# A planned order set to measured durations of products, and the decay matrices moved from VectorE to GpSimd and ScalarE

## The reference

```python
# first block
h = rms_norm(x); (aq,ak,av,az,dq,dk,dv,db,da,dz,gate_att,gate_dn) = split_cols(h @ w_in)
y_att = (gqa_attention(rope(norm(aq)), rope(norm(ak)), av) * silu(az)) @ w_br_att     # 8 heads, 2 kv heads
qkv = silu(short_conv([dq,dk,dv]))                                                      # 5 taps
g = -exp(a_log) * softplus(da + dt_bias); beta = sigmoid(db)                            # 2 directions, 8 heads
o_dn = gated_delta(q,k,v,g[0],beta[0]) + flip(gated_delta(flip q,k,v,g[1],beta[1]))     # chunks
  # in it: g = cumsum(g) per chunk
  #        decay = exp(where(tril, g[:, None] - g[None, :], -inf))
  #        L = tril((k_beta @ k.T) * decay, -1); T = (I + L)^-1; u, w, a_intra = (q @ k.T) * decay; scan over chunks
y_dn = (rms_norm(o_dn) * silu(dz)) @ w_br_dn
x = x + rms_norm((sigmoid(gate_att)*y_att + sigmoid(gate_dn)*y_dn) @ w_out)
x = x + rms_norm(sigmoid(x @ w_ple_gate) * (p @ w_ple_proj))
# second and third block
x = x + stick_breaking_attention(...)@w_out;  x = x + swiglu_ffn(rms_norm(x))           # 16 heads
x = x + (rms_norm(a1@v - lam*a2@v) per head)@w_out;  x = x + swiglu_ffn(rms_norm(x))    # differential attention, 8 heads
```

## Time and profile before

| | value |
|---|---|
| median of 3 runs (range) | 2147.75 us (2145.37 to 2148.02) |
| the profiled execution's own time | 2149.83 us |
| its span | 2148.0 us |
| granted clock of TensorE, mean | 0.997 |
| PE busy | 2104.3 us, 98% |
| DVE busy | 1275.4 us, 59% |
| ACT busy | 1054.6 us, 49% |
| POOL busy | 235.0 us, 11% |
| share of the ending chain: PE, DVE, ACT, issue | 89%, 6%, 3%, 1% |

### The profile page before, as it was taken

The page is one execution under the profiler, slowest core; times in us unless marked ns, Lnnn a source line. Parts: engine busy times, 40 slices in busy tenths (PEclk is TensorE's granted clock), DMA queues, the critical chain, the costliest instruction groups (busy, mean ns, idle before and its releaser), DMA issues.

```text
span 2148.0 us, 36022 instructions
## 1 busy us (share of the span) xinstructions
PE 2104.3 (98%) x15046; PEld 1680.9 (78%) x15046; DVE 1275.4 (59%) x2281; ACT 1054.6 (49%) x2046; POOL 235.0 (11%) x240
## 2 busy tenths in 40 slices
PE   7999999999999999999999999999999999999999
PEld 6777777787778887877777888888777777888887
DVE  6777677776755455655567443444577775443442
ACT  6656766676655236656665332323455554222331
POOL 1013222231210011100001000000100101000000
PEclk9999999999999999999999999999999999999999
DMA  4321212222224332111111332222221212232222
GB/s 179 108 75 62 77 68 85 68 77 65 71 80 147 127 137 95 60 59 59 59 59 64 101 114 81 98 98 98 84 64 64 64 59 99 98 103 94 98 100 77
DMA packets 36227, 186.76 MB, mean 87 GB/s; under 512 B 4560, under 2 KB 4944, under 8 KB 16992
## 3 DMA queue, kind: packets, MB, share of 16 engines
q1 hardware_dynamic: 36064, 184.45, 25.1%
HBM read 172.86 MB, written 7.90 MB: 84 GB/s over the span
## 4 chain that ended last, share of the span: by engine, by line
PE 89%; DVE 6%; ACT 3%; issue 1%; DMA 0%; SPq 0%; POOL 0%; DVEq 0%; ACTq 0%
PE ps L1879 87%; ACT arena L2841 1%; PE ps L1882 1%; DVE spl L2337 1%; ACT spl L2844 1%; ACT hh L2841 0%; DVE x L2706 0%; DMA raw<-wstream 0%; DVE x L2464 0%; DVE arena L2356 0%; DVE arena L2649 0%; DVE x L2635 0%; DVE arena L2631 0%; DVE hl L2657 0%; DVE hl L2639 0%
## 5 line engine op out<-in xcount | busy, mean ns | idle before, releaser
L1879 PE MATMUL ps<-hh,spl 128*128 128x512 f32 (+1 forms) x3152 | 1018.2, 396 | 10.9 <-ACT x L2844 2.1
L1879 PEld LDWEIGHTS ps<-hh,spl 128*128 128x128 f32 x3152 | 584.7, 189 | 144.7 <-issue 19.1
L1879 PE MATMUL ps<-hl,spl 128*128 128x512 f32 (+1 forms) x1568 | 616.0, 393 | 0.0
L2337 DVE TENSOR_TENSOR spl<-raw,spl 128x512 fp32r<-128x512 f32 x596 | 427.2, 740 | 159.1 <-ACT spl L2844 158.0
L1879 PE MATMUL ps<-arena_r,spl 128*128 128x512 f32 x1968 | 468.7, 393 | 10.4 <-DVE arena_r L2349 8.5
L1879 PEld LDWEIGHTS ps<-arena_r,spl 128*128 128x128 f32 x1968 | 371.9, 189 | 90.1 <-issue 10.9
L2844 ACT ACTIVATE spl<-raw 128x512 fp32r<-128x512 f32 x596 | 345.1, 619 | 144.4 <-PE ps L1879 138.2
L1879 PEld LDWEIGHTS ps<-hl,spl 128*128 128x128 f32 x1568 | 295.5, 188 | 60.6 <-issue 4.8
L2841 ACT ACTIVATE arena<-arena 128x512 f32<-128x512 f32 (+3 forms) x220 | 142.2, 648 | 187.3 <-DVE arena L2711 141.1
L1879 PE MATMUL ps<-arena 32*32 32x32 f32 (+5 forms) x5664 | 216.9, 224 | 7.5 <-issue 6.1
L1879 PEld LDWEIGHTS ps<-arena 32*32 32x32 f32 (+4 forms) x5664 | 126.1, 115 | 82.3 <-issue 70.6
(11 more groups left out here) (271 smaller groups left out, 2143.1 us busy)
## 6 DMA issues: line engine op xcount, KB each, us to landing
raw<-wstream SPq DMA_DIRECT2D x148, 1024.0 KB, 4.9
arena<-spill SPq DMA_DIRECT2D x17, 256.0 KB, 4.5
GS<-g_rows SPq DMA_DIRECT2D x16, 256.0 KB, 3.3
spill<-x SPq DMA_DIRECT2D x14, 256.0 KB, 2.6
arena<-arena SPq DMA_DIRECT2D x18, 128.0 KB, 2.0
x<-xT SPq DMA_DIRECT2D x4, 512.0 KB, 6.2
spill<-arena SPq DMA_DIRECT2D x8, 256.0 KB, 2.1
x<-xT SPq DMA_DIRECT2D x1, 2048.0 KB, 8.3
```

Source lines behind the costliest of these rows:

```text
L1879: return pe.matmul(out, lhsT, rhs, start=start, stop=stop, skip_group_check=True)
L2337: tt(spl[:, p % 2, 1, c], raw[:, p % 2, c], spl[:, p % 2, 0, c].bitcast(F32), ALU.subtract) \
```

## The change

Two parts. **First**, constants of the planner's clock. `CHANGE` was one number between "one pass" products and others; it becomes a table over three forms of product, WIDE (512 columns on the whole array), NARROW (128 columns) and TILED (parts of the array). The costs of about fifteen steps are set to other values, and three base values. **Second**, the decay matrices. Before, VectorE computed min(g_j - g_i, 0) with four TENSOR_SCALARs for each head and direction, ScalarE one exp over 128x512, and GpSimd multiplied by a triangular mask (L3278). After, GpSimd adds a mask of 0 and -1e30 to g_j (one instruction), and ScalarE computes exp(x - g_i) in four ACTIVATEs of 128x128 that take -g_i as bias; the gate column is negated once. The small copy `eglast` moves on GpSimd from `pr_e` to `pr_q`, and the scan's state update waits for `pr_q` in place of `pr_e`. The GpSimd step gets two new waits, since it now writes the buffers: for `pr_b` of the head before, and for the drained bank of `lv_q2` two heads back.

```diff
-PE_B, DV_B, AC_B, PO_B = 0.86, 0.69, 0.62, 1.25
-PE_S2 = 0.46
+PE_B, DV_B, AC_B, PO_B = 0.866, 0.69, 0.62, 1.25
+PE_S2 = 0.47
-PE_H, DV_H, AC_H = 0.44, 0.41, 0.37
+PE_H, DV_H, AC_H = 0.35, 0.41, 0.37
-CHANGE = 0.088
-ONE_PASS = ("mul", "tok", "ar_ss", "cv_r", "on_b", "st_w", "st_t")
+CHANGE = {(WIDE, TILED): 0.1, (NARROW, TILED): 0.1, (TILED, WIDE): 0.1, (TILED, NARROW): 0.05, (NARROW, WIDE): 0.06}
...
-            st = banked("df_s", m, qb, cost=[("PE", 0.15 + 0.86 * f), ("DV", 0.15 + 1.08 * f), ("AC", 0.25 + 0.42 * f),
+            st = banked("df_s", m, qb, cost=[("PE", 0.25 + 0.85 * f), ("DV", 0.15 + 1.08 * f), ("AC", 0.25 + 0.42 * f),
...
@@ rows_lane
-            yield "DV"
+            yield "AC"
             o.add("pr_a", hd, d, cost=[("AC", AC_B)])
-            yield "DV"
-            o.add("pr_g", hd, d, cost=[("DV", 4 * DV_S)]).ib = decays[hd]
+            yield
+            o.add("pr_g", hd, d, cost=[("PO", 1.4)]).ib = decays[hd]
...
-            yield
-            o.add("pr_e", hd, d, cost=[("AC", AC_B), ("PO", PO_B)]).ib = decays[hd]
+            yield "AC"
+            o.add("pr_e", hd, d, cost=[("AC", 4 * 0.36)]).ib = decays[hd]
@@ vector
-                elif kind == "pr_g":
-                    hd, d = q.key
-                    col = d * 8 + hd
-                    w.wait_ge(sem(f"g_ld{d}"), 16 * (hd + 1))
...
-                    for c in range(4):
-                        i = ts(g4(B_of[q.ib][d])[:, c, :], g4(GS[:, d, :])[:, c, :], g3(gcol)[:, c, col:col + 1], 0.0,
-                               ALU.subtract, ALU.min)
-                    i.then_inc(sem("pr_d"), 1)
...
-                        w.wait_ge(sem("pr_ld"), at["pr_e", hd, 1].n)
+                        w.wait_ge(sem("pr_qe"), at["pr_q", hd, 1].n)
@@ scalar, pr_e
-                    f(B_of[q.ib][d], B_of[q.ib][d], ACT.Exp).then_inc(sem("pr_ed"), 1)
...
+                    for c in range(4):
+                        b_, col = g4(B_of[q.ib][d])[:, c, :], d * 8 + hd
+                        i = f(b_, b_, ACT.Exp, bias=g3(gcol)[:, c, col:col + 1])
+                    i.then_inc(sem("pr_ld"), 1)
@@ gpsimd
-                elif kind == "pr_e":
+                elif kind == "pr_g":
                     hd, d = q.key
-                    e0, D = (d * 8 + hd) * 4, B_of[q.ib][d]
-                    w.wait_ge(sem("pr_eg"), at["pr_a", hd, d].n)
-                    po.tensor_copy(eglast[:, e0:e0 + 4], g4(G_of[d])[:, :, 127 if d == 0 else 0])
-                    w.wait_ge(sem("pr_ed"), q.n)
-                    tt(g4(D), g4(D), bc4(C["tri_u" if d == 0 else "tri_l"]), ALU.mult).then_inc(sem("pr_ld"), 1)
+                    w.wait_ge(sem(f"g_ld{d}"), 16 * (hd + 1))
+                    if hd > 1:
+                        w.wait_ge(sem("pr_b"), hd - 1)
+                        t = at["lv_q2", hd - 2].u
+                        w.wait_ge(drained[t.b], t.n)
+                    tt(g4(B_of[q.ib][d]), g4(GS[:, d, :]), bc4(C["off_u" if d == 0 else "off_l"]), ALU.add) \
+                        .then_inc(sem("pr_d"), 1)
```

More of the change, by code:

```diff
@@ L44 @@
 NVEC = _at
-PE_B, DV_B, AC_B, PO_B = 0.86, 0.69, 0.62, 1.25
-PE_S2 = 0.46
+PE_B, DV_B, AC_B, PO_B = 0.866, 0.69, 0.62, 1.25
+PE_S2 = 0.47
 PE_S, DV_S, AC_S, PO_S = 0.21, 0.34, 0.3, 0.6
 MUL, MUL_H = 0.228, 0.117
-PE_H, DV_H, AC_H = 0.44, 0.41, 0.37
+PE_H, DV_H, AC_H = 0.35, 0.41, 0.37
 HOP = 0.08
-CHANGE = 0.088
-ONE_PASS = ("mul", "tok", "ar_ss", "cv_r", "on_b", "st_w", "st_t")
+WIDE, NARROW, TILED = 0, 1, 2
+CHANGE = {(WIDE, TILED): 0.1, (NARROW, TILED): 0.1, (TILED, WIDE): 0.1, (TILED, NARROW): 0.05, (NARROW, WIDE): 0.06}
+FORM = {**dict.fromkeys(("at_o", "at_t", "sc_r", "sc_v", "sc_oq", "sc_s", "sc_o", "tr_k", "tr_v", "pr_kk", "df_t", "df_o"),
+                        NARROW),
+        **dict.fromkeys(("lv_m", "lv_x", "lv_p1", "lv_p2", "lv_q1", "lv_q2", "st_z", "st_o", "df_s"), TILED)}
 TAIL_32 = 0.4
@@ L141, in __init__ @@
         self.uses, self.fills, self.bank_free = [0] * 8, [0] * 8, [0.0] * 8
-        self.forced, self.aside = False, False
+        self.forced, self.form = False, WIDE
         self.lanes, self.later = {}, []
@@ L161, in add @@
             st.u, t = u, max(t, u.t)
-        if cost and cost[0][0] == "PE" and self.aside != (kind not in ONE_PASS):
-            self.aside = not self.aside
-            self.clock["PE"] += CHANGE
+        if cost and cost[0][0] == "PE":
+            form = FORM.get(kind, WIDE)
+            self.clock["PE"] += CHANGE.get((self.form, form), 0.0)
+            self.form = form
         for q, c in cost:
@@ L573, in att_lane @@
             if qb:
-                banked("at_t", hd, qb - 1, cost=[("PE", 0.45), ("AC", AC_B)])
+                banked("at_t", hd, qb - 1, cost=[("PE", 0.43), ("AC", AC_B)])
                 o.now = t
@@ L690, in conv_lane @@
                 yield "PE"
-            st = banked("tr_k", hd, cost=[("PE", 0.45), ("AC", AC_B)])
+            st = banked("tr_k", hd, cost=[("PE", 0.44), ("AC", AC_B)])
             st.keep = kept[hd]
@@ L742, in prep_lane @@
             yield "PE"
-        st = add("pr_kk", hd, cost=[("PE", 1.7), ("DV", 2 * DV_B), ("DV", 8 * DV_S)], hold=True)
+        st = add("pr_kk", hd, cost=[("PE", 1.82), ("DV", 2 * DV_B), ("DV", 8 * DV_S)], hold=True)
         st.u2 = ring.take()
@@ L801, in scan_lane @@
             if s > 0:
-                add("sc_r", s, [("PE", 0.43), ("DV", 2 * DV_S)])
+                add("sc_r", s, [("PE", 0.44), ("DV", 2 * DV_S)])
                 yield "PE"
             t = o.now
-            add("sc_v", s, [("PE", 0.43), ("AC", 0.72)])
+            add("sc_v", s, [("PE", 0.44), ("AC", 0.72)])
             if s > 0:
                 t, o.now = o.now, t
-                st = add("sc_oq", s, [("PE", 0.43)], False)
+                st = add("sc_oq", s, [("PE", 0.55)], False)
                 st.first, first, o.now = first, False, max(t, o.now)
@@ L812, in scan_lane @@
             if s < 3:
-                add("sc_s", s, [("PE", 0.43), ("DV", 2 * DV_S)])
+                add("sc_s", s, [("PE", 0.44), ("DV", 2 * DV_S)])
             t, o.now = o.now, t
-            st = add("sc_o", s, [("PE", 0.43)], False)
+            st = add("sc_o", s, [("PE", 0.46)], False)
             st.first, first, o.now = first, False, max(t, o.now)
@@ L1328, in stick_back @@
             z = o.at["st_z", m, kb]
-            st = last = o.add("st_w", m, kb, cost=[("PE", 0.1 + 0.92 * f)])
+            st = last = o.add("st_w", m, kb, cost=[("PE", max(0.45, 0.93 * f))])
             st.ih = o.at["st_h", m, kb].ih
@@ L1334, in stick_back @@
                 ut = obs.take()
-                last = o.add("st_t", m, kb, cost=[("PE", 0.1 + 0.92 * f)], u=ut)
+                last = o.add("st_t", m, kb, cost=[("PE", max(0.45, 0.93 * f))], u=ut)
                 last.u, last.isp, last.ih = ut, z.isp, st.ih
@@ L1509, in mix_lane @@
         yield "AC PE"
-        st = banked("df_o", m, cost=[("PE", 2.2), ("AC", AC_B), ("AC", AC_B)], bank=obk)
+        st = banked("df_o", m, cost=[("PE", 2.12), ("AC", AC_B), ("AC", AC_B)], bank=obk)
         st.iat, st.old = iat, on_old
@@ L3284, in gpsimd @@
                     w.wait_ge(sem("cv_n"), at["cv_n", hd].n)
-                    tt(keep_of[q.keep][f"qe{d}"], q_tile[hd % 2], G_of[d], ALU.mult).then_inc(sem("pr_qe"), 1)
+                    po.tensor_copy(eglast[:, e0:e0 + 4], g4(LG)[:, :, 127 if d == 0 else 0])
+                    tt(keep_of[q.keep][f"qe{d}"], q_tile[hd % 2], LG, ALU.mult).then_inc(sem("pr_qe"), 1)
                 elif kind == "lv_0":
@@ L3349, in shape_constants @@
          "neg_ones": -np.ones((128, 128), np.float32), "strict_u": one(r < c), "neg_lo": -1e30 * one(c >= r % 64),
-         "neg_hi": -1e30 * one(c >= 64 + r % 64), "rep64": one(c == r % 64)}
+         "neg_hi": -1e30 * one(c >= 64 + r % 64), "rep64": one(c == r % 64),
+         "off_u": -1e30 * one(r > c), "off_l": -1e30 * one(r < c)}
     lev = []
```

14 lines of the change are left out of this document (8 added, 6 removed).

## The result

The changed kernel takes 2170.73 us (median of 5 runs, 2167.0 to 2176.54) against 2148.02; the ratio is 1.0106, 95% interval 1.0093 to 1.0118. It is 22.7 us slower. 2155 was forecast and 2167 was the upper end: the direction was right, the size a third of what came. The profiled execution of the changed kernel took 2176.54 (span 2174.8), the slowest of the five, so a comparison of the two traces has 26.7 us to explain.

A forecast was written before the change was run, and what follows sets the result against it. TensorE, busy for 2104.3 of 2148.0 us, was taken as the bound, so only its gaps counted. The terms summed to +7.6: 2157.4 for the profiled execution, 2155 us against the medians, range 2146 to 2167.

The forecast's parts named there:

- B: End of the last differential head: its chain loses 41 output-projection products as cover; +6.1 us (4.7 to 7.6).
- A: First block, successive projections on one bank: six turn-arounds instead of four, one long at head 5; +4.0 us (0 to +9).
- C: Before the fourth output block: fewer products stand beside the chain from norm's sum to split; +1.5 us (0 to 3.0).
- F: First block's decay matrices: relief of VectorE removes half of its gaps; -2.5 us (-4.6 to +4.5).
- G: Gaps with no semaphore, in runs of 32x32 products: denser runs add +1.3 us (-7.8 to +6).
- D: End of the stick-breaking attention: eight products fill TensorE's wait of 1.85; -1.8 us (-1.85 to 0).
- E: Changes between forms of product: fall from 702 to 680 in the written order; -1.0 us (-2 to 0).
- The larger rival: First block: exps with waits precede most bank-emptying steps, GpSimd beside VectorE costs time; +17 us, about 2164; chance 0.21.

The follow-up runs named there:

- d_only: The kernel before with only the new decay matrices and those steps' own planner costs; all other planner costs old: 2147.27 us, ratio 0.9995.
- tail_only: The kernel before with only the end of the last differential head moved behind the 41 products of the output projection: 2156.48 us, ratio 1.0036.
- b_late_new: The kernel before with the new product costs from the differential attention (third block) on: 2157.46 us, ratio 1.0051.
- p_only: The kernel before with only the planner's new costs of products and changes of form; decay matrices computed as before: 2162.65 us, ratio 1.0062.

## Why the prediction was wrong in size

The sum was +7.6; the run gave +22.7 by the medians and +26.7 between the two traces, by which the terms are read here.

- **B, the last head, +6.1: right as a wait (5.98, in four pieces of which the last has 3.55), short as a cost, 10.0.** The sum priced waits by their length. The half clock behind the last of them adds 2.7, four stops and starts 1.3.
- **The half clock in the first block, in no term: up to +5.1.** This is the step that failed most plainly, together with B's: the clock was taken as full behind every new wait, without a reason, though the earlier trace rows showed six products in 2.20 us behind a wait of 1.85.
- **A, +4.0: +8.0.** The long turn-around of head 5 came as priced (3.13 for 3.5). The other five were taken at 0.69 each, as where ScalarE's queue is empty; they were 2.58, 0.69, 0.93, 0.65 and 1.26, and one product behind a bank of longer ago waited 1.61. Between 60 and 700 ScalarE's waits are 10.8 against 2.8. d_only also has six turn-arounds on one bank, with waits of 0 to 0.82, and lost nothing: their number was the wrong measure, what stands in the queue before the emptying is the right one.
- **C, +1.5 (0 to 3.0): a wait of 2.35, 2.5 from start to start.** B and C are 10.0 + 2.5 = 12.5 of the 12.7 between 1792 and 1870.
- **F, -2.5: -0.4.** VectorE's waits between 60 and 700 went from 4.8 to 4.4, though VectorE has less to do (20.5 us less busy over the whole kernel). Relief on average did not reach the instructions that TensorE waits for, and at projection 64 one of them took 1.1 longer beside GpSimd. The prediction had that contention in F's upper bound, at 0.28 an instruction, a quarter of what the pair above shows.
- **G, +1.3: +2.0** (7.8 to 9.8). Within its bounds; the order of before also shows 8.7 and 8.8 in other traces, so little of it is certain.
- **D, -1.8: -3.3.** The wait of 1.85 is gone, and with it 1.6 of half clock that the trace before happened to have there and tail_only and b_late_new, behind the same wait, did not.
- **E, -1.0:** nothing in the runs tells it apart.

The larger rival (2164) was nearest. Of its two mechanisms GpSimd beside VectorE exists; but a `pr_e` stands in front of only one of the six turn-arounds, and not of most. The half clock was in neither forecast, and with A at 4.0 in place of 8.0 it is why 2167 was too low an upper end. By the medians the 22.7 are: the third block's order 9.6 and the rest of the new costs 5.1 (p_only 14.7), the decays' instructions in that order 3.3, and 4.8 for the order that the decays' costs bring. What stays open is that last part: it shows as waits on ScalarE and VectorE spread over heads 0 to 5, one attempt to mend it at two places moved them, and no single step was found that makes it.

## What to carry to other kernels

Price a wait of TensorE of 3 us or more at its length plus 1 to 2.6 us of half clock, one of 2 to 2.6 as likely to bring it as not, and look for slow products behind the waits that the trace already has. Count slow products from start to start, and each once: two waits with few products between them have one slow stretch. When a planner's costs change, count for each chain the products left beside it in the written order: 41 or none at one place decided about 8 us, though no product's cost in the planner had moved by more than 0.15. Before giving GpSimd an instruction that reads SBUF, look at what VectorE does at that moment: the work moved off VectorE can come back as longer instructions there.

## What the hardware showed unexpectedly

Delays of very different length brought a similar half clock: 13 slow products behind 3.2 us, 6 behind 13.9. The same wait of 2.35 us was followed by the half clock in five traces and not in three. And a VectorE multiplication of 0.68 us took 1.77 beside a GpSimd addition of 1.73 and 1.68 beside one of 1.26, but 0.69 beside a fill of 0.53.
